# A three-layer transformer step: weight halves behind the norms, context keys and values beside a norm, q's second chunk rotated beside the first heads

## The chip, the cores and the metric

The kernel runs on one core of one Trainium2 chip. It is timed as a whole: device microseconds of one execution, median of several runs.

## The reference

An input of 256 tokens by 1024 goes through two layers and then through a third with a context of another 256 tokens:

```python
h = h + mix(rms_norm(h))         # layer a: dilated window attention; layer b: gated linear attention
h = h + swiglu(rms_norm(h))      # each with a gated FFN behind it
...
hx = modulate(rms_norm_2(x), sh1, sc1);  hc = modulate(rms_norm_2(ctx), csh1, csc1)
k_x = apply_axial_rope(rms_norm_2(ak_x), cos, sin);  k_c = rms_norm_2(ak_c)      # 2 key heads of 128
q_x = apply_axial_rope(rms_norm_2(aq_x), cos, sin)                               # 8 query heads of 128
attn_x = softmax(q_x @ [k_c, k_x].T / sqrt(128)) @ [v_c, v_x]
```

The third layer adds a gated delta rule (GDN) over context and input, merges the two, and ends in an FFN with a short convolution. Context and input use the same weight columns for keys and values. All matrices are fp32.

## The kernel before

Every product is made of three TensorE products in a rounded format (`mm3`, lines 324 to 326): operands are split in a high part (rounded on ScalarE) and a low part (the rest, on VectorE). Weights come in halves of 4 x 128 rows by 512 columns. `Weights` streams them in one fixed order: `load` on the SP queue into 4 raw buffers, `hi` (line 189) on ScalarE into 3 high buffers, `lo` (line 195) on VectorE in place of the raw half. `hi` of half h waits until half h - 3 is used up, `load` until half h - 4 is. A chunk is two halves (512 weight columns). `chunk_tok` multiplies a chunk for tiles of 128 tokens (tiles 0 and 1 the input's, 2 and 3 the context's), 12 products of 512 columns per half and tile.

No order is planned by a program: each engine works through its instructions as they are written, and semaphores join the engines. `Stage()` notes the newest signal of each engine when it is made, and `meet(engine)` makes an engine wait for all of them; every stage begins with it.

A *seam* is the piece between two layers. The last chunk of a stage is multiplied tile by tile (`last_tok`, or the end of `ffn`), so that the norm of tile 0 can start before tile 1 is done. `Norm.on_act` (line 525 squares, 527 root) and `Norm.on_dve` (532 reciprocal, 534 scale) stand behind the residual add of each tile (line 582 behind a mixer, 757 behind an FFN). Both halves of the next product (`nxt`) are rounded and split ahead of that, on ScalarE and on VectorE. Then `Norm.split` transposes the normed tiles on TensorE (line 405) into PSUM banks 4 to 7, after a wait for the last add, and splits them (ScalarE 423 or 414, VectorE 436, 443 or 452). Behind layer a, `GateWeights` is set up between the seam and the FFN: four DMA issues on ScalarE and a memset (line 1267) on VectorE; the stage of the FFN is noted behind it. Beside the FFN of layer b, `ContextNorm` norms and splits the context.

`attention_2` is the attention of the third layer. Chunk 0 gives keys and values for all four tiles (banks 0 to 3), chunks 1 and 2 give q (banks 4 to 7). Each is normed per head and rotated (`HeadNorm`): squares on ScalarE (856), sums (869), root (861), reciprocal (874), scale (878) and sine products (887) on VectorE, cosine products (900) and the add (905) on GpSimd. All three use the same buffers, so the squares of one wait for the add of the one before. Then comes a stage (`mid`), and behind it the heads: transposes of the keys (1688), a staging copy (1750), transposes of q (1725), and 16 units of scores (1697), maximum (1764, 1766), exponential (1744), transposes (1705), copy (1785, reciprocal 1786), values (1714) and result (1772). The units are in two groups of eight; the second group's q is copied, transposed and copied (1777) between them. The first two halves of the next stage, `gdn_inputs`, are rounded and split beside the q rotations.

## Time and profile before

| | |
|---|---|
| median of 3 runs | 1977.47 us (1976.63 to 1977.7) |
| the profiled execution | 1972.33 us |
| its span, first to last instruction | 1971.0 us |
| mean granted TensorE clock | 0.936 |
| TensorE products busy | 1701.1 us (86%), 10106 instructions |
| VectorE, ScalarE, GpSimd busy | 1143.7, 860.3, 238.5 us |
| DMA | 240.97 MB, mean 122 GB/s |

The profile is that of one execution. In a timeline row the first number is the start (us from the span's start), the second the time, and in brackets stand the engine's idle time ahead of it and what ended that. PE is the matrix engine TensorE, DVE VectorE, ACT ScalarE, POOL GpSimd. A window row gives the stretch, its length, the busy time of PE, PEld (weight loads), DVE, ACT and POOL with the number of instructions, then the granted TensorE clock, the share of DMA and GB/s.

### The profile page before, as it was taken

To read this page: it belongs to the slowest core of one execution; us is meant where nothing else is said; L and a number is where in the kernel's file an instruction comes from. 1 tells how busy PE (TensorE), PEld (TensorE's weight loads), DVE (VectorE), ACT (ScalarE), POOL (GpSimd) and SP (SyncE) were. 2 spreads that over 40 slices of the span, in tenths; PEclk is the share of its full clock that TensorE was granted. 3 is DMA by queue.
4 is the path that set the end of the run, shared out by engine and by line. 5 is a ranking of instruction groups with operands and counts; after the bars stand their busy time and mean duration, and the time that the engine had idled before them with its cause. 6 is when DMAs were issued, how large, how long until landed. Compare 5 with 4: busy or idle time off the path is not lost. (4 is left out here: it accounts for less than half of the span.)

```text
span 1971.0 us, 25094 instructions
## 1 busy us (share of the span) xinstructions
PE 1701.1 (86%) x10106; PEld 1479.6 (75%) x10106; DVE 1143.7 (58%) x1466; ACT 860.3 (44%) x1055; POOL 238.5 (12%) x200
## 2 busy tenths in 40 slices
PE   3998999879997986689997689967979979979988
PEld 2777888869986864579985568746979858769976
DVE  2887666745544456545544664427888555547754
ACT  4435556634434452344443234335544444335543
POOL 1553230000000000000001400002553200000000
PEclk9999999979998898789998889987989889989999
DMA  4553335536544352245543304100000055435533
GB/s 164 169 179 107 129 129 193 192 102 191 184 169 160 117 169 99 78 156 182 184 162 97 126 1 114 60 0 17 1 1 1 1 174 179 161 122 184 175 140 118
DMA packets 161906, 240.97 MB, mean 122 GB/s; under 512 B 12640, under 2 KB 80992, under 8 KB 161664
## 3 DMA queue, kind: packets, MB, share of 16 engines
q1 hardware_dynamic: 154400, 232.81, 36.2%
q10 hardware_dynamic: 7248, 5.77, 1.0%
q8 instruction: 81, 1.33, 0.3%
q0 software_dynamic: 144, 0.79, 0.1%
q14 instruction: 33, 0.27, 0.0%
HBM read 238.29 MB, written 1.05 MB: 121 GB/s over the span
## 5 line engine op out<-in xcount | busy, mean ns | idle before, releaser
L195 DVE TENSOR_TENSOR wlo<-raw,whi 128x2048 fp32r<-128x2048 f32 x224 | 523.9, 2351 | 361.7 <-ACT whi L189 348.5
L189 ACT ACTIVATE whi<-raw 128x2048 fp32r<-128x2048 f32 x224 | 420.1, 1886 | 352.3 <-PE ps L326 308.7
L324 PE MATMUL ps<-xs,whi 128*128 128x256 f32 (+1 forms) x1312 | 388.1, 296 | 17.7 <-DVE xs L443 5.1
L325 PE MATMUL ps<-xs,whi 128*128 128x256 f32 (+1 forms) x1312 | 386.5, 295 | 0.0
L326 PE MATMUL ps<-xs,wlo 128*128 128x256 f32 (+1 forms) x1312 | 386.2, 294 | 0.0
L324 PE MATMUL ps<-whi,xs 128*128 128x512 f32 x672 | 275.0, 409 | 35.3 <-DVE wlo L195 19.5
L324 PEld LDWEIGHTS ps<-xs,whi 128*128 128x128 f32 x1312 | 251.3, 192 | 27.3 <-issue 20.8
L325 PE MATMUL ps<-wlo,xs 128*128 128x512 f32 x672 | 269.6, 401 | 0.0
L326 PE MATMUL ps<-whi,xs 128*128 128x512 f32 x672 | 269.5, 401 | 0.0
L325 PEld LDWEIGHTS ps<-xs,whi 128*128 128x128 f32 x1312 | 251.3, 192 | 5.7
L326 PEld LDWEIGHTS ps<-xs,wlo 128*128 128x128 f32 x1312 | 251.0, 191 | 5.8
L324 PEld LDWEIGHTS ps<-whi,xs 128*128 128x128 f32 x672 | 129.3, 192 | 68.3 <-issue 36.7
L326 PEld LDWEIGHTS ps<-whi,xs 128*128 128x128 f32 x672 | 128.8, 192 | 32.0
L325 PEld LDWEIGHTS ps<-wlo,xs 128*128 128x128 f32 x672 | 129.3, 192 | 28.7
L324 PE MATMUL ps<-whi,hid 128*128 128x512 f32 x264 | 106.0, 402 | 8.7 <-DVE wide L728 8.7
L326 PE MATMUL ps<-whi,hid 128*128 128x512 f32 x264 | 105.5, 399 | 0.0
L325 PE MATMUL ps<-wlo,hid 128*128 128x512 f32 x264 | 105.4, 399 | 0.0
L1659 POOL TENSOR_TENSOR wide<-cst,wide 128x128 f32<-128x128 f32 x4 | 3.5, 863 | 789.5 <-DMA wide<-in_rows 789.5
L900 POOL TENSOR_TENSOR wide<-wide 128x512 f32<-128x512 f32 (+1 forms) x32 | 56.8, 1795 | 154.6 <-DVE wide L887 83.5
L905 POOL TENSOR_TENSOR wide<-wide 128x512 f32<-128x512 f32 (+1 forms) x32 | 72.1, 2275 | 3.4 <-DVE wide L887 2.4
L324 PEld LDWEIGHTS ps<-whi,hid 128*128 128x128 f32 x264 | 50.4, 191 | 21.0 <-DVE wide L728 9.1
L400 PE MATMUL ps<-cst,wide 128*128 128x128 f32 x112 | 20.0, 355 | 48.5 <-DVE wide L476 28.8
(360 smaller groups left out, 2423.9 us busy)
## 6 DMA issues: line engine op xcount, KB each, us to landing
raw<-in_ffn_w_gate_up SPq DMA_DIRECT2D x88, 512.0 KB, 4.7
raw<-in_a_w_in SPq DMA_DIRECT2D x72, 512.0 KB, 4.6
raw<-in_w_in SPq DMA_DIRECT2D x60, 512.0 KB, 4.6
raw<-in_w_mod SPq DMA_DIRECT2D x48, 512.0 KB, 4.6
raw<-in_w_up SPq DMA_DIRECT2D x44, 512.0 KB, 4.7
raw<-in_ffn_w_down SPq DMA_DIRECT2D x40, 512.0 KB, 4.5
raw<-in_b_w_in SPq DMA_DIRECT2D x24, 512.0 KB, 4.6
raw<-in_w_down SPq DMA_DIRECT2D x20, 512.0 KB, 3.9
```

Source lines behind the costliest of these rows:

```text
L189: self.hi_ok.inc(act.activation(self.whi[:, h % NHI, 0:nk, :], self.raw[:, h % NRAW, 0:nk, :], ACT.Copy))
L195: self.lo_ok.inc(dve.tensor_tensor(self.wlo[:, h % NRAW, 0:nk, :], self.raw[:, h % NRAW, 0:nk, :], self.whi[:, h % NHI, 0:nk, :].bitcast(F ...
L324: pe.matmul(o, ahi, bhi, start=start, stop=False)
L325: pe.matmul(o, ahi, blo, start=False, stop=False)
L326: return pe.matmul(o, alo, bhi, start=False, stop=stop)
L400: i_ = pe.transpose(ps[:, self.bank + g, (j * 2 + t) * P:(j * 2 + t + 1) * P], self.src(t, 2 * g + j), ident)
L900: i_ = pool.tensor_tensor(self.av[:, t], self.xv[:, t], bc(cos[:, t, :], 1, self.nh), ALU.mult)
L905: i_ = pool.tensor_tensor(dst(t), self.av[:, t], dst(t) if self.bv is None else self.bv[:, t], ALU.add)
L1659: pool.tensor_tensor(tab[:, 0, t, :], cosv[:, t, :], gain, ALU.mult)
```

## The change

At the seams, the second half of the next chunk is rounded behind the norm of both tiles and its low half is taken behind the split; `Norm` gets a bank of its own (4 for four of the norms, 0 for that between layer a's FFN and layer b), and the wait for the last add goes away, except in the seam ahead of the third layer. The FFN of layer a gets a stage that is noted ahead of `GateWeights`.

In the seam ahead of the third layer the products of the context's two tiles with the two halves of chunk 0 are made inside the seam (`context_first`): those with the first half ahead of the transposes, those with the second behind them. The low half of the second weight half is taken ahead of the split there. `attention_2` then makes only the input's two tiles of chunk 0.

In `attention_2` the three rotations get buffers of their own; the stage `mid` goes; the keys are transposed between the two halves of chunk 2; the first group of heads waits only for q's first chunk, and q's second chunk is rotated beside it: its cosine and sine products and the add on GpSimd. The 16 units run through, with the staging copy of the second group at unit 6 and its transposes and copy around units 6 and 7. The second half of the next stage is rounded behind the first staging copy and its low half taken in unit 2. What is computed stays the same. The core of the diff:

```diff
@@ -333,8 +333,10 @@
-    def chunk_tok(chunk, banks, tiles=(0, 1)):
-        for s, half in enumerate(chunk):
+    def chunk_tok(chunk, banks, tiles=(0, 1), parts=(0, 1), keep=False):
+        for s in parts:
+            half = chunk[s]
...
-            W.used.inc(i_)
+            if not keep:
+                W.used.inc(i_)
             self.root, self.ready = [0, 0], [0, 0]
-        def split(self):
-            parts = Split(lambda t, k: self.xn[:, t, k * P:(k + 1) * P], 0, self.stage, self.scale, self.shift, self.perm)
-            pe.wait_ge(added.sem, added.n)
+        def split(self, last, ahead=None):
+            parts = Split(lambda t, k: self.xn[:, t, k * P:(k + 1) * P], 0, self.stage, self.scale, self.shift, self.perm, self.bank)
+            if ahead is not None:
+                ahead(0)
+                pe.wait_ge(added.sem, added.n)
             for t in range(TT):
                 pe.wait_ge(st_ready.sem, self.ready[t])
                 parts.tile_on_pe(t)
+            W.hi(last)
             parts.on_act()
-            parts.on_dve()
+            if ahead is not None:
+                ahead(1)
+                W.lo(last)
+                parts.on_dve()
+            else:
+                parts.on_dve()
+                W.lo(last)
...
@@ -553,7 +568,7 @@
         def on_act():
-            for h in (*chunks[1], *nxt):
+            for h in (*chunks[1], nxt[0]):
-            for h in nxt:
-                W.lo(h)
+            W.lo(nxt[0])
...
         yb, zb = (c(2, 4, SEQ), c(2, 4, SEQ)) if conv is not None else (None, None)
-        at_, a0, v0, h0, l0, m0, y0 = Stage(), ff_act.n, ff_val.n, ff_hi.n, ff_lo.n, ff_y0.n, ff_y.n
-        order = [*up[1:], *down[0], *down[1], nxt]
+        at_ = at_ or Stage()
+        a0, v0, h0, l0, m0, y0 = ff_act.n, ff_val.n, ff_hi.n, ff_lo.n, ff_y0.n, ff_y.n
+        order = [*up[1:], *down[0], *down[1], nxt[:1]]
-        def squares(self, u, x):
-            if u:
+        def squares(self, u, x, own=False):
+            if u and not own:
                 act.wait_ge(hr_out.sem, u)
+            if sin is None:
+                return
...
+    def context_first(chunk, split, s):
+        pe.wait_ge(xs_hi.sem, split.hi0 + 4)
+        pe.wait_ge(xs_lo.sem, split.hi0 + 4)
+        want = list(xs_want)
+        xs_want[:] = [0, 0]
+        chunk_tok(chunk, (2, 3), (2, 3), (s,), keep=True)
+        xs_want[:] = want
...
+        def turned_on_pool():
+            r = rope_q[1]
+            pool.wait_ge(hr_xn.sem, x0 + 3)
+            for t in range(TT):
+                i_ = pool.tensor_tensor(r.av[:, t], r.xv[:, t], bc(tq[:, 0, t, :], 1, 4), ALU.mult)
+            hr_a.inc(i_)
+            for t in range(TT):
+                for c0 in (0, 64):
+                    halves = r.xv[:, t, :, c0:c0 + 64].rearrange("p h (s n) -> p h s n", s=2)[:, :, ::-1, :]
+                    i_ = pool.tensor_tensor(r.bv[:, t, :, c0:c0 + 64].rearrange("p h (s n) -> p h s n", s=2), halves,
+                                            bc(tq[:, 1, t, c0:c0 + 64], 1, 4).rearrange("p h (s n) -> p h s n", s=2), ALU.mult)
+            hr_a.inc(i_)
+            pool.wait_ge(hr_a.sem, a0 + 4)
+            for t in range(TT):
+                i_ = pool.tensor_tensor(q_to(1, t), r.av[:, t], r.bv[:, t], ALU.add)
+            hr_out.inc(i_)
+        def on_pe():
+            at_.meet(pe)
+            chunk_tok(chunks[0], (0, 1), (0, 1))
+            chunk_tok(chunks[1], (4, 5))
+            chunk_tok(chunks[2], (6, 7), parts=(0,))
+            pe.wait_ge(hr_out.sem, out0 + 1)
+            pe.wait_ge(c2_v.sem, 1)
             for g in range(KV2):
                 for t in range(NT2):
                     i_ = pe.transpose(ps[:, g, t * P:(t + 1) * P], k[:, t, g * HD2:(g + 1) * HD2], ident)
             c2_kt.inc(i_)
+            chunk_tok(chunks[2], (6, 7), parts=(1,))
+            q_transposes(0)
+            pe.wait_ge(c2_k.sem, 1)
+            scores(0)
+            for u in range(16):
+                if u < 15:
+                    scores(u + 1)
+                transposes(u)
+                if u:
+                    values(u - 1)
+                if u == 6:
+                    q_transposes(1)
+            values(15)
+        def q_transposes(g):
+            pe.wait_ge(c2_st.sem, g + 1)
+            pe.wait_ge(c2_k.sem, g)
+            for t in range(TT):
+                for h in range(GROUP2):
+                    i_ = pe.transpose(ps[:, 4 * (1 - g) + t, h * P:(h + 1) * P], stg[:, t, h * P:(h + 1) * P], ident)
+            c2_qt.inc(i_)
...
+        def values(u):
+            g, par = u // 8, u % 2
+            pe.wait_ge(c2_etv.sem, u + 1)
+            if u < 2:
+                pe.wait_ge(hr_xn.sem, x0 + 3)
+            else:
+                pe.wait_ge(c2_out.sem, u - 1)
+            for j in range(NT2):
+                i_ = pe.matmul(ps[:, 6 + par, 0:P], ET[:, par, j * P:(j + 1) * P], v[:, j, g * HD2:(g + 1) * HD2],
+                               start=(j == 0), stop=(j == NT2 - 1))
...
+        def on_act():
+            at_.meet(act)
+            load_row(gk, "k_norm")
+            load_row(gq, "q_norm")
+            for h in chunks[1]:
+                W.hi(h)
+            W.wait_used(act, chunks[0][1])
+            rope_k.on_act(u0, ps[:, 0:4, 0:256])
+            act.wait_ge(hr_xn.sem, x0 + 1)
+            c2_v.inc(act.activation(v, ps[:, 0:4, 256:512], ACT.Copy))
+            for h in chunks[2]:
+                W.hi(h)
+            W.wait_used(act, chunks[1][1])
+            rope_q[0].squares(u0 + 1, q_of(0), own=True)
+            rope_q[0].root(u0 + 1)
+            W.hi(nxt[0])
+            act.wait_ge(hr_out.sem, out0 + 2)
+            c2_st.inc(act.activation(stg, q[:, :, 0:CW], ACT.Copy))
+            W.hi(nxt[1])
+            W.wait_used(act, chunks[2][1])
+            rope_q[1].squares(u0 + 2, q_of(1), own=True)
+            rope_q[1].root(u0 + 2)
+            for u in range(16):
+                if u == 6:
+                    act.wait_ge(hr_out.sem, out0 + 3)
+                    act.wait_ge(c2_qt.sem, 1)
+                    c2_st.inc(act.activation(stg, q[:, :, CW:2 * CW], ACT.Copy))
+                exponentials(u)
+        def on_dve():
+            at_.meet(dve)
+            for h in chunks[1]:
+                W.lo(h)
+            dve.wait_ge(c2_tab.sem, 1)
+            rope_k.on_dve(u0, ps[:, 0:4, 0:256], tk[:, 1])
+            for h in chunks[2]:
+                W.lo(h)
+            rope_q[0].on_dve(u0 + 1, q_of(0), tq[:, 1])
             dve.wait_ge(c2_kt.sem, 1)
             c2_k.inc(dve.tensor_copy(kT, ps[:, 0:2, :]))
+            W.lo(nxt[0])
+            rope_q[1].sums(u0 + 2)
+            rope_q[1].scale_and_sin(u0 + 2, q_of(1), None)
+            dve.wait_ge(c2_qt.sem, 1)
+            c2_q.inc(dve.tensor_copy(qT[:, 0], ps[:, 4:6, :]))
+            maxima(0)
+            for u in range(16):
+                par, n = u % 2, u % 8
+                if u == 7:
+                    dve.wait_ge(c2_qt.sem, 2)
+                    c2_q.inc(dve.tensor_copy(qT[:, 1], ps[:, 0:2, :]))
+                if u < 15:
+                    maxima(u + 1)
+                dve.wait_ge(c2_et.sem, u + 1)
+                dve.wait_ge(c2_exp.sem, u + 1)
+                dve.tensor_copy(ET[:, par, :], ps[:, 4 + par, :])
+                c2_etv.inc(dve.reciprocal(rl[:, n:n + 1], l[:, n:n + 1]))
+                if u == 2:
+                    W.lo(nxt[1])
+                if u:
+                    result(u - 1)
+            result(15)
...
-    layer_a(N["a_in"], N["a_out"], N["ffn_a"][0][0], Norm(4096, f_norm[:, 0, :]))
+    layer_a(N["a_in"], N["a_out"], N["ffn_a"][0][0], Norm(4096, f_norm[:, 0, :], bank=4))
+    ffn_stage = Stage()
     gw = GateWeights()
-    ffn(*N["ffn_a"], N["b_in"][0], Norm(3072, a_norm[:, 1, :]), beside=gw)
-    layer_b(N["b_in"], N["b_out"], N["ffn_b"][0][0], Norm(0, f_norm[:, 1, :]), gw)
+    ffn(*N["ffn_a"], N["b_in"][0], Norm(3072, a_norm[:, 1, :]), beside=gw, at_=ffn_stage)
...
-    ffn(*N["ffn_b"], N["akv"][0], Norm(3072, modcol[:, 1, :, 0], modcol[:, 0, :, 0]), beside=ContextNorm(ctx))
+    cn = ContextNorm(ctx)
+    ffn(*N["ffn_b"], N["akv"][0], Norm(3072, modcol[:, 1, :, 0], modcol[:, 0, :, 0], bank=4), beside=cn,
+        ahead=lambda s: context_first(N["akv"][0], cn.split, s))
```

In the lines left out, `exponentials`, `maxima`, `result`, `scores` and `transposes` are the functions of before, moved; `q_transposes` writes banks 4 and 5 for the first group, 0 and 1 for the second; and the other calls of `Norm` get `bank=4`.

## Rows read from the trace of the kernel before

**Rows 1.** The page of the kernel before: granted TensorE clock in its 40 slices

```profile
PEclk9999999979998898789998889987989889989999
```

**Rows 2.** The list of waits, TensorE: who was waited for, us in total, times, longest

```profile
PE ps L405 <- DVE resid L582: 20.1, 3, 8.1
...
PE ps L1688 <- POOL wide L905: 18.0, 1, 18.0
```

**Rows 3.** The timeline (start, us) and a window row, the fifth seam

```profile
1051.29 1.92 ACT L189 ACTIVATE whi<-raw 128x2048 fp32r<-128x2048 f32 x1 [5.12 <-PE ps L326]
...
1053.30 2.29 DVE L195 TENSOR_TENSOR wlo<-raw,whi 128x2048 fp32r<-128x2048 f32 x1 [4.74 <-ACT whi L189]
...
1058.60 0.68 DVE L757 TENSOR_TENSOR resid<-resid,ps 128x512 f32<-128x512 f32 x1
...
1059.34 1.97 PE L405 MATMUL ps<-cst,wide 128*128 128x128 f32 x8 [6.75 <-DVE resid L757]
...
1066.19 2.48 DVE L443 TENSOR_TENSOR xs<-wide,xs 128x512 fp32r<-128x512 f32 x4
...
1068.88 0.76 PE L324 MATMUL ps<-whi,xs 128*128 128x512 f32 x1 [5.08 <-DVE xs L443]
...
1068.90:1073.00 4.10, 4.10 (x10) 3.23 (x11) 1.19 (x1) 1.91 (x1) 0.69 (x1) 0.51 0.13 32
```

**Rows 4.** The timeline, TensorE: transposes and restart at the other four seams

```profile
425.03 1.97 PE L405 MATMUL ps<-cst,wide 128*128 128x128 f32 x8 [6.63 <-DVE resid L582]
...
433.93 0.55 PE L324 MATMUL ps<-xs,whi 128*128 128x256 f32 x1 [4.44 <-DVE wide L1267]
...
632.86 1.97 PE L405 MATMUL ps<-cst,wide 128*128 128x128 f32 x8 [8.03 <-DVE resid L757]
...
640.38 0.39 PE L324 MATMUL ps<-xs,wzs 128*32 128x256 f32 x1 [3.06 <-DVE xs L452]
...
850.69 1.97 PE L405 MATMUL ps<-cst,wide 128*128 128x128 f32 x8 [5.35 <-DVE resid L582]
...
858.22 0.55 PE L324 MATMUL ps<-xs,whi 128*128 128x256 f32 x1 [3.32 <-DVE xs L452]
...
1748.96 1.97 PE L405 MATMUL ps<-cst,wide 128*128 128x128 f32 x8 [8.09 <-DVE resid L582]
...
1758.50 0.55 PE L324 MATMUL ps<-xs,whi 128*128 128x256 f32 x1 [5.08 <-DVE xs L443]
```

**Rows 5.** The timeline and a window row: projections and rotations of the attention

```profile
1093.39 1.03 ACT L856 ACTIVATE wide<-ps 128x1024 f32<-128x1024 f32 x1 [9.23 <-PE ps L326]
...
1101.61 5.03 DVE L195 TENSOR_TENSOR wlo<-raw,whi 128x2048 fp32r<-128x2048 f32 x2
...
1112.94 3.63 DVE L887 TENSOR_TENSOR wide<-wide 128x256 f32<-128x256 f32 x4
...
1116.71 6.45 POOL L905 TENSOR_TENSOR wide<-wide 128x512 f32<-128x512 f32 x2 [0.76 <-DVE wide L887]
...
1131.15 2.48 POOL L905 TENSOR_TENSOR wide<-wide 128x512 f32<-128x512 f32 x2 [0.76 <-DVE wide L887]
...
1093.40:1115.60 22.20, 22.20 (x96) 17.66 (x94) 17.05 (x23) 10.88 (x9) 12.45 (x10) 1.00 0.59 190
```

**Rows 6.** The timeline: the 16 units of the heads, and the stage behind them

```profile
1140.48 2.08 PE L1697 MATMUL ps<-wide 128*128 128x512 f32 x2 [1.31 <-DVE wide L1777]
...
1145.14 0.69 DVE L1785 COPY wide<-ps 128x512 f32<-128x512 f32 x1
...
1149.29 0.69 DVE L1785 COPY wide<-ps 128x512 f32<-128x512 f32 x1
...
1158.06 0.69 DVE L1785 COPY wide<-ps 128x512 f32<-128x512 f32 x1
...
1167.46 0.69 DVE L1785 COPY wide<-ps 128x512 f32<-128x512 f32 x1 [0.70 <-PE ps L1705]
...
1184.28 0.36 PE L324 MATMUL ps<-xs,whi 128*128 128x256 f32 x1 [0.60 <-PE ps L1714]
```

More of the change, by code:

```diff
@@ L624, in build, with ffn @@
     DOWN = ((0, (HK, HK)), (8, (HK, HK)), (16, (HK, 2)))
-    def ffn(up, down, nxt, norm, conv=None, gate=None, beside=None):
+    def ffn(up, down, nxt, norm, conv=None, gate=None, beside=None, at_=None, ahead=None):
         c = Carve(end=arena_n - 2 * FT * SEQ)
@@ L762, in ffn @@
         on_dve()
-        norm.split()
+        norm.split(*nxt[1:], **({} if ahead is None else {"ahead": ahead}))
     md_sil, md_hi, md_rows = (Signal(nc, "act", "mod_" + n) for n in ("silu", "hi", "rows"))
@@ L1241, in split_and_add @@
         prod_dve()
-        norm.split()
+        norm.split(nxt[1])
     lb_w = Signal(nc, "dma", "b_gate_weights")
@@ new lines, in scores, with transposes @@
+        def scores(u):
+            g, h, t, par = u // 8, u % 8 // 2, u % 2, u % 2
+            if u % 8 < 2:
+                pe.wait_ge(c2_q.sem, g + 1)
+            if u >= 2:
+                pe.wait_ge(c2_exp.sem, u - 1)
+            c2_sc.inc(pe.matmul(ps[:, 2 + par, :], qT[:, g, t, h * P:(h + 1) * P], kT[:, g, :], start=True, stop=True))
+        def transposes(u):
+            par = u % 2
+            pe.wait_ge(c2_exp.sem, u + 1)
+            if u >= 2:
+                pe.wait_ge(c2_etv.sem, u - 1)
+            for j in range(NT2):
+                i_ = pe.transpose(ps[:, 4 + par, j * P:(j + 1) * P], E[:, par, j * P:(j + 1) * P], ident)
+            c2_et.inc(i_)
```

188 lines of the change are left out of this document (46 added, 142 removed).

## The prediction

> **What bounds the kernel now.** I read the page first: the clock line of its slices [rows 1] shows TensorE at its upper level wherever it is kept busy, and below it only in some slices. So TensorE is the bound, except where it waits. The list of TensorE's waits [rows 2] shows on whom: 20.1 us in three waits of the norms' transposes (line 405) for the residual add of line 582 (two more, for the add of line 757, are like it), and 18.0 us in one wait of the attention's first transposes (line 1688) for GpSimd's last rope add. Then I read the timeline at these places. There are five seams, where a layer's last product is added, normed, transposed, split and only then multiplied: layer a to its FFN, that to layer b, b to its FFN, that to the keys and values of the context layer, and the mixer c to its FFN.
>
> **How a seam works** [rows 3, 4]. At 1051.29 ScalarE rounds the *second* weight half of the next product. It could not start earlier: its buffer is that of the last product's first half. The squares of token tile 0 are queued behind it, VectorE's low half (1053.30, 2.29 us) too, although the products of tile 0 were done 18 products before the end. The add of tile 1 follows at 1058.60, 6.0 us after the last product ended (1059.34 less 6.75 is 1052.6). TensorE starts again at 1068.88, at half clock: the granted clock is 0.51 for 4.1 us, that is 1.2 GHz. 96 products at the full pace (22.20 us for 96, 0.231 each, [rows 5]) would take 22.3 us; these end at 1093.3, after 24.4. So the restart costs 2 us more.
>
> **The change, part by part: four seams.** The second half moves behind the norm (rounding on ScalarE, low half behind the split on VectorE); the transposes go to banks that nobody reads, so tile 0's no longer wait for the add of tile 1. Tile 0's chain (add, squares, root, scale; 3.1 us, 4.4 with a table load, longer by two products with the gate in c) now runs beside tile 1's products, and the add of tile 1 starts about 0.2 us after the last product. In [rows 4] the transposes start 0.73 us behind that add, so it starts at 424.3, 632.1, 850.0, and with c's gate (one product more) 1747.5; the last products ended at 418.4, 624.8, 845.3 and 1740.9. In the seam to layer b tile 0's chain is late: add at 620.8, done at 625.4, so the second add starts there 0.5 us behind the products. It comes earlier by 5.7, 6.8, 4.4 and 6.4 us. Against this: every later stage waits for the *newest* signal of each engine. Behind the split that is now the low half of 2.29 us, so TensorE's restart pays it in full: the wait that takes the place of the one removed. ScalarE's rounding (1.9 us) holds the split up by 0.15, and nothing in c. In the first seam the stage of the FFN is noted ahead of the gate weights, so the memset (the wait of 4.44 us on line 1267) no longer stands before TensorE: 1.4 us. Net: 5.7 - 2.3 - 0.2 + 1.4 = 4.6; 6.8 - 2.3 - 0.2 = 4.3; 4.4 - 2.3 - 0.1 = 2.0; 6.4 - 2.3 = 4.1. Sum 15.0 us. The half clock after each restart I leave as it is: pauses of 5.3 us bring it already [rows 4], and about 6 us of waiting remain. If one such restart were spared it would give 2 us; so 0 to 8 more.
>
> **The fifth seam** also gets work. Of the 96 products of the first chunk 48 are for the context, whose split is long done. 24 (5.6 us) stand ahead of the transposes, 24 behind them. From 1052.6: products to 1058.2. The add of tile 1 is at 1052.8 and its chain done at 1056.0, rounding to 1057.0, low half to 1059.4 (ahead of the split here): all covered. The transposes (16, 2.0 us at full clock, 3.9 at half) 1058.2 to 1060.3; modulation and split on VectorE, 3.7 + 2.5 us as now, to 1065.8; beside them the other 24 products to 1065.9. TensorE thus never pauses long enough to lose its clock. The 48 latent products end at 66.0 + 11.2 = 1077.3 instead of 1093.4: 16.1 us earlier. Uncovered, the first 24 would cost up to the 2.2 us by which they outlast the norm; that is in the sum.
>
> **From there to the first score.** Now it takes 1140.5 - 1093.4 = 47.1 us. Keys and values keep their course [rows 5]: squares, root, scale, sine, and VectorE's two low halves end 13.2 us behind the chunk, so at 1090.5. TensorE meanwhile has chunk 1 (11.1 us, to 1088.5) and half of chunk 2 (to 1094.1); the low half of that is due at 1088.2, which is just in time (0 to 1 us). The first q squares have buffers of their own and no longer wait for GpSimd's add: sums start at 1090.6, where they started 3.2 us behind the low halves before. Sums to the end of the sine take 6.8 us: 1097.4. Then GpSimd's add. Alone the pair takes 2.48 us; beside two low halves it took 6.45; now a copy and one low half run beside it: I take 4.5, the middle, so 1102.1, with 2.5 and 6.5 as ends. Staging copy 1.06, transposes 1.0. ScalarE, behind the copy, rounds a half (1.9) and squares q's second chunk (1.03); VectorE sums, root, reciprocal, scale (3.1): 1109.3; its copy of the turned q 1.22; first score at 1110.7. From the chunk's end that is 33.4 us instead of 47.1: 13.7 us saved.
>
> **The heads.** 16 units; VectorE is the bound in each, the copies of line 1785 at 1149.29 and 1158.06 are four units apart, 2.19 us each [rows 6]. Between the groups the pipeline drains: 1145.14 to 1167.46 is 22.3 us for 8 units, 4.8 more than 17.5. In its place come a copy of 1.22 and one score that it holds up, about 2.1: a gain of 2.7; the low half moved into unit 2 costs 2.3. Net 0.4 us. GpSimd now turns q's second chunk itself: 3 us of cosines, 4 sine products that no row shows on it. Nearest: its cosine product of the same 128x256 shape, 0.78 us; at the worst 1.7, its add of that shape beside low halves. So 3 to 7 us, then the add, 2.5 to 6.5: done between 1118 and 1126. ScalarE asks for it at unit 6, at 1110.7 + 2.1 + 13.1 + 2.3 = 1128.2. Hidden, with 2 us to spare at the worst by these rows.
>
> At this add a rule of the Trainium skill bears (SBUF — State Buffer, section Who interferes with whom): a VectorE instruction with two SBUF inputs and a GpSimd one that reads SBUF exclude each other for a whole instruction. This trace agrees (6.45 against 2.48 us). By that rule the add waits out one low half, 2.48 + 2.3 = 4.8, and the sum is 0.3 us smaller.
>
> A rule that speaks against moving the sine: GPSIMD Engine Reference, section Performance versus the Vector engine, gives tensor_tensor on GpSimd as 1.96 times as long as on VectorE. VectorE's four sine products take 3.6 us here, so by that page 7.1 us, an estimate; the sum would stay, and the spare at unit 6 is what it eats.
>
> **Sum:** 15.0 + 16.1 + 13.7 + 0.4 = 45.2 us. The profiled execution took 1972.3 us (span 1971.0 and 1.3 around it), so 1927.1 for its like; the median of the runs is 5.1 us above it, so 1932.3 for the median. That is the forecast.
>
> **The rivals.** (1) *Unit 6 waits for GpSimd.* For it: no row shows the reversed product there, and the add beside VectorE takes up to 3.2 us an instruction. If all eight instructions took 3.3 us, it would end at 1109.3 + 26.4 = 1135.7, ScalarE's copy at 1136.8, and the heads would stand for 8.5 us: 1941. Against it: the cosines took 1.5 each. (2) *The context products are not hidden* (the low half late, or the norm behind them): half of them, 5.6, to all, 11.2 us, come back: 1938 to 1943.5. Against it: the working above, with 0.9 us between low half and the end of the transposes. (3) *The clock is spared* at the seams: two to four restarts without the half clock, 4 to 8 us more: 1924 to 1928. For it: transposes of tile 0 follow the products at once. Against it: 6 us of waiting remain. (4) *The seams give nothing*, as the low half and the rounding eat all: 1947. Against it: they cost 2.4 of 4.4 to 6.8. (5) *Slower:* the granted clock. TensorE's rests go away; if the chip answered more work with its lower level for longer, each 1% of mean clock would cost about 17 us (1701 us busy). From a mean of 0.91 instead of 0.936 on it would eat the gain, at 0.90 the kernel would be slower, near 1990. Against it [rows 1, 5]: the clock is 1.00 in all stretches where TensorE has been busy throughout. (6) *The change doesn't do what it says*: another stage still waits on a newer signal. Within 0.2%, 1977.
>
> **How the numbers follow.** Forecast 0.66, (1) 0.09, (2) 0.07, (3) 0.10, (4) 0.04, (5) 0.02, (6) 0.02. Bounds of the unknown costs around 1932.3: down 2.0 (the add alone), 8 (clock), 2 (noise); up 2.0 (the add), 1 (first half of chunk 2), 2 (four seams), 2 (noise), 5 (pipeline of the heads disturbed by copy, transposes and low half). They are not all due at once; together with rivals (1) to (3) the range 1921 to 1944 leaves about 2 in 10 out. A measurement here can tell about 0.2%, 4 us. Faster by more: all but (5) and (6), 0.96; within: 0.02; slower: 0.02.
>
> **What would show it.** In the new trace: at four seams the add of tile 1 within 1 us of the last product, and TensorE released not by the split but by the low half (line 195); if it is released by the split, the seam gains 2.3 more. In the fifth no pause above 1 us and clock 1.00 through it. The first score 33 us behind the chunk's end, released by VectorE's copy. Unit 6 and 7 without a wait on GpSimd. Units still at 2.19 us. The forecast is wrong if a unit lengthens, if GpSimd's second rotation takes over 19 us, or if the mean clock falls.

## The result, and the profile of the changed kernel

The changed kernel takes 1928.33 us (median of 4 executions, 1925.72 to 1930.22), the kernel before beside it 1977.05. The ratio is 0.9753, with an interval of 0.9736 to 0.977: between 45.5 and 52.2 us less, 48.7 by the medians. Forecast were 1932.3 in a range of 1921 to 1944. The profiled execution took 1925.72 us, its span 1924.4 (before 1971.0: 46.6 less); the sum of the prediction was 45.2.

Where the 46.6 us lie, place by place in the two traces (all in us):

| place | before | after | gain | predicted |
|---|---|---|---|---|
| seam a to FFN, last product's end to restart | 15.53 | 10.42 | 5.1 | 4.6 |
| seam to layer b | 15.55 | 10.64 | 4.9 | 4.3 |
| seam b to FFN | 12.87 | 10.42 | 2.45 | 2.0 |
| seam c to FFN | 17.62 | 13.00 | 4.6 | 4.1 |
| fifth seam, last product's end to the first chunk's end | 40.8 | 24.8 | 16.0 | 16.1 |
| chunk's end to first score | 47.1 | 33.1 | 14.0 | 13.7 |
| first score to the stage behind the heads | 43.8 | 43.4 | 0.4 | 0.4 |
| everything the change doesn't touch | | | -0.8 | 0 |

The page of the changed kernel, its busy times, then its granted clock in 40 slices, which answers to [rows 1]:

```profile
PE 1689.2 (88%) x10106; PEld 1470.5 (76%) x10106; DVE 1138.4 (59%) x1462; ACT 859.3 (45%) x1055; POOL 240.9 (13%) x204
...
PEclk9999999989999898789999899978989989989989
```

What went is mostly waiting: of the 46.6 us, 34.7 are idle time of TensorE and 11.9 busy time (1701.1 us before). The same 10106 products took less because more of them ran at the upper clock; between the last product of the FFN and the end of the first chunk of the fifth seam alone TensorE was busy for 28.5 us before and for 24.6 after. The list of TensorE's waits of the changed kernel (who was waited for, us in total, times, longest), which answers to [rows 2]:

```profile
PE ps L324 <- DVE wlo L195: 47.5, 18, 13.6
...
PE ps L408 <- DVE wide L538: 10.3, 5, 3.1
...
PE ps L1733 <- DVE wide L1808: 6.0, 1, 6.0
```

The waits of the transposes for the residual add and of the heads for GpSimd are gone. In their place stand the low half of line 195 (22.9 us in 14 waits before), the last scale of the norm (line 538) and VectorE's copy of the turned q (line 1808).

One of the four seams, layer a to its FFN, in the timeline of the changed kernel (start, duration, engine, line, operation; in brackets the idle time before and who ended it), which answers to [rows 4]:

```profile
421.98 1.04 PE L408 MATMUL ps<-cst,wide 128*128 128x128 f32 x8
...
422.18 0.69 DVE L596 TENSOR_TENSOR resid<-resid,ps 128x512 f32<-128x512 f32 x1 [1.07 <-PE ps L326]
...
424.28 1.90 ACT L189 ACTIVATE whi<-raw 128x2048 fp32r<-128x2048 f32 x1
...
425.41 1.22 PE L408 MATMUL ps<-cst,wide 128*128 128x128 f32 x8 [2.40 <-DVE wide L538]
...
426.93 3.22 DVE L455 SCALAR_TENSOR_TENSOR xs<-ps,vec,xs 128x256 fp32r<-128x256 f32 x8 [1.57 <-ACT xs L426]
...
430.07 2.28 DVE L195 TENSOR_TENSOR wlo<-raw,whi 128x2048 fp32r<-128x2048 f32 x1
...
432.56 0.55 PE L324 MATMUL ps<-xs,whi 128*128 128x256 f32 x1 [5.93 <-DVE wlo L195]
```

Tile 0's transposes run as the last products end (422.14), with the add of tile 1 beside them and not in front of them. The rounding fits between the norm's root and the transposed values. The split is done at 430.15, and TensorE could go; it goes 2.4 us later, released by the low half. The other three seams end in the same way. The transposes of tile 0 and the restart in the seam to layer b, and the restart in c's:

```profile
623.79 1.09 PE L408 MATMUL ps<-cst,wide 128*128 128x128 f32 x8 [0.41 <-DVE wide L538]
...
634.03 0.39 PE L324 MATMUL ps<-xs,wzs 128*32 128x256 f32 x1 [5.85 <-DVE wlo L195]
...
1710.80 0.55 PE L324 MATMUL ps<-xs,whi 128*128 128x256 f32 x1 [7.90 <-DVE wlo L195]
```

The fifth seam of the changed kernel, timeline and then a window row (stretch, its length, busy time and count of PE, PEld, DVE, ACT and POOL, granted clock, DMA share, GB/s), which answer to [rows 3]:

```profile
1042.83 0.69 DVE L773 TENSOR_TENSOR resid<-resid,ps 128x512 f32<-128x512 f32 x1 [0.96 <-PE ps L326]
...
1046.95 2.29 DVE L195 TENSOR_TENSOR wlo<-raw,whi 128x2048 fp32r<-128x2048 f32 x1 [0.92 <-ACT whi L189]
...
1048.25 1.91 PE L408 MATMUL ps<-cst,wide 128*128 128x128 f32 x16
...
1055.96 0.47 PE L324 MATMUL ps<-whi,xs 128*128 128x512 f32 x1 [0.18 <-issue]
...
1042.60:1056.00 13.40, 13.22 (x66) 10.61 (x64) 10.01 (x16) 5.79 (x8) 0.00 (x0) 1.00 0.46 156
```

TensorE is busy for 13.22 of 13.40 us between the last product of the FFN and the first of the latents, at a clock of 1.00, and the rest of the chunk, to 1067.4, has 1.00 too. Before, that stretch was a pause, and the restart ran at 0.51.

From the chunk's end to the first score, timeline of the changed kernel, which answers to [rows 5] and the first of [rows 6]:

```profile
1063.86 2.93 POOL L1666 TENSOR_TENSOR wide<-cst,wide 128x32 f32<-128x32 f32 x4
...
1067.43 1.03 ACT L872 ACTIVATE wide<-ps 128x1024 f32<-128x1024 f32 x1 [3.62 <-PE ps L326]
...
1068.79 1.22 DVE L885 TENSOR_REDUCE wide<-wide 128x8 f32<-128x1024 f32 x1 [2.52 <-POOL wide L1669]
...
1083.97 3.62 DVE L905 TENSOR_TENSOR wide<-wide 128x256 f32<-128x256 f32 x4
...
1087.73 4.57 POOL L923 TENSOR_TENSOR wide<-wide 128x512 f32<-128x512 f32 x2 [0.77 <-DVE wide L905]
...
1088.65 2.53 DVE L195 TENSOR_TENSOR wlo<-raw,whi 128x2048 fp32r<-128x2048 f32 x1
...
1099.16 1.21 DVE L1808 COPY wide<-ps 128x1024 f32<-128x1024 f32 x1
...
1100.52 3.75 PE L1733 MATMUL ps<-wide 128*128 128x512 f32 x4 [5.99 <-DVE wide L1808]
```

And the second rotation, which now runs on GpSimd beside the first heads, with ScalarE's copy of its result for unit 6:

```profile
1099.32 2.48 POOL L1680 TENSOR_TENSOR wide<-wide 128x512 f32<-128x512 f32 x2 [7.02 <-DVE wide L894]
...
1101.76 2.77 POOL L1685 TENSOR_TENSOR wide<-wide 128x256 f32<-128x256 f32 x4
...
1104.61 2.49 POOL L1690 TENSOR_TENSOR wide<-wide 128x512 f32<-128x512 f32 x2
...
1115.86 1.05 ACT L1782 ACTIVATE wide<-wide 128x1024 f32<-128x1024 f32 x1
```

It takes 7.8 us in all and is done at 1107.1, 8.8 us before it is asked for.

### The profile page after: what moved, and what is told of

It reads as the page before. It is cut to its first block and busy times, and to the rows that moved or that the text cites. A ratio compares the mean times of both kernels' runs of the same rounds, so it can differ in the third digit from the quotient of the medians.

```text
span 1924.4 us, 25090 instructions
## 1 busy us (share of the span) xinstructions
PE 1689.2 (88%) x10106; PEld 1470.5 (76%) x10106; DVE 1138.4 (59%) x1462; ACT 859.3 (45%) x1055; POOL 240.9 (13%) x204
## 5 line engine op out<-in xcount | busy, mean ns | idle before, releaser
L324 PE MATMUL ps<-whi,xs 128*128 128x512 f32 x672 | 275.9, 411 | 29.5 <-DVE wlo L195 18.7
L918 POOL TENSOR_TENSOR wide<-wide 128x512 f32<-128x512 f32 (+1 forms) x30 | 54.0, 1822 | 135.0 <-DVE wide L905 83.2
L923 POOL TENSOR_TENSOR wide<-wide 128x512 f32<-128x512 f32 (+1 forms) x30 | 67.7, 2280 | 2.6 <-DVE wide L905 1.7
```

What stands on the lines that cost most here:

```text
L324: pe.matmul(o, ahi, bhi, start=start, stop=False)
L918: i_ = pool.tensor_tensor(self.av[:, t], self.xv[:, t], bc(cos[:, t, :], 1, self.nh), ALU.mult)
L923: i_ = pool.tensor_tensor(dst(t), self.av[:, t], dst(t) if self.bv is None else self.bv[:, t], ALU.add)
```

## The experiments

Each edit is one to the changed kernel, unless it says otherwise. The ratio is the kernel's time over that of the kernel before, run on the same chip; the changed kernel itself has 0.9753, and 0.9752 with an interval of 0.9737 to 0.9766 when it was run again.

### Does each part give what the trace says?

**The four seams as before** (both halves ahead of the norm, the old wait, the stage noted behind the gate weights; the fifth seam and the attention stay changed):

```
-                pe.wait_ge(added.sem, added.n)
+            pe.wait_ge(added.sem, added.n)
...
-            W.hi(last)
+            if ahead is not None:
+                W.hi(last)
...
-                W.lo(last)
...
-            for h in (*chunks[1], nxt[0]):
+            for h in (*chunks[1], *nxt):
...
-            W.lo(nxt[0])
+            for h in nxt:
+                W.lo(h)
...
-        order = [*up[1:], *down[0], *down[1], nxt[:1]]
+        order = [*up[1:], *down[0], *down[1], nxt if ahead is None else nxt[:1]]
...
-    ffn(*N["ffn_a"], N["b_in"][0], Norm(3072, a_norm[:, 1, :]), beside=gw, at_=ffn_stage)
+    ffn(*N["ffn_a"], N["b_in"][0], Norm(3072, a_norm[:, 1, :], bank=4), beside=gw)
```

> The changed kernel with four seams as before (both halves of the next chunk ahead of the norm, a wait for the last add, layer a's FFN noted behind its gate weights); the fifth seam and the attention stay changed. Theory: the seams gave 16.6 us in the trace (last product to restart: 15.5, 15.6, 12.9, 17.6 us before, 10.6, 10.7, 10.6, 13.2 after), so 1928.3 + 16.6 = 1945. Rival (seam times are luck of the clock, the rest of the stages gives it back): under 1938.

Measured: 1946.26 us, ratio 0.9852 (0.9839 to 0.9866). The four pauses are 15.49, 15.54, 12.90 and 17.64 us, as before; all 17.1 us are back. By the ratios it is 0.0099, 19.5 us; their intervals leave about 15 to 24. So the seams give what the traces show, some 17 us, and nothing else in the kernel gives it.

**The context products back behind the norm.** No products run ahead in the fifth seam, and the attention's first chunk has all 96 again:

```
             if ahead is not None:
-                ahead(0)
                 pe.wait_ge(added.sem, added.n)
...
-                ahead(1)
                 W.lo(last)
...
-            chunk_tok(chunks[0], (0, 1), (0, 1))
+            chunk_tok(chunks[0], (0, 1, 2, 3), (0, 1, 2, 3))
```

> The changed kernel with the context's 48 products back in the attention's first chunk. Theory: they cost their 11.2 us, and TensorE's pause of some 10 us in the seam brings the half clock back for 2 us: 1928.3 + 13.2 = 1941.5; the restart stays 13.2 to 13.4 us behind the last product, as the low half and VectorE's split set it. Rival (the products delayed the norm, so taking them out lets TensorE restart 2.2 us earlier): 1939. Rival (they were not hidden): within 5 us of 1928.

Measured: 1937.85 us, ratio 0.9812 (0.9797 to 0.9828), 0.0059 above the changed kernel: 11.7 us. Its timeline, restart and chunk's end:

```profile
1053.64 0.76 PE L324 MATMUL ps<-whi,xs 128*128 128x512 f32 x1 [7.42 <-DVE xs L446]
...
1078.25 1.03 ACT L870 ACTIVATE wide<-ps 128x1024 f32<-128x1024 f32 x1 [9.22 <-PE ps L326]
```

The last product of the FFN ends at 1040.97 here; the restart comes 12.67 us behind it, 0.7 earlier than with the context products between, and then at half clock: 24.6 us for 96 products where the full pace is 22.3. The chunk ends 37.3 us behind the last product instead of 24.8. So 12.5 of the 16 us are the filled pause with its spared restart. The other 3.5 are what the rest of the change gives in this seam, the second half rounded behind the norm; this part is the difference, and no run takes it back alone. The expectation of 13.2 left out the 0.7 us that the restart comes earlier when no context products stand in front of the transposes; its rival had 2.2 us for that.

**The heads wait for q's second chunk again.** How much of the attention's gain is that they no longer do? The first transposes of q wait again until the rotation of the *second* chunk is done too:

```
             pe.wait_ge(c2_st.sem, g + 1)
+            if g == 0:
+                pe.wait_ge(hr_out.sem, out0 + 3)
```

> The changed kernel, but TensorE turns the first q chunk only when GpSimd has rotated the second one too (one wait more). Theory: GpSimd's last add ends 7.8 us behind VectorE's scaling of the second chunk, at 1107.1 in the trace; transposes (1 to 2 us), copy 1.2: first score at 1109.4 to 1110.5 instead of 1100.5, so 9 to 10 us more: 1938. Rival (the first score waits mainly for something else, the copy or ScalarE): under 4 us more.

Measured: 1936.7 us, ratio 0.9803 (0.9783 to 0.9823). In its timeline:

```profile
1102.39 1.94 PE L1726 MATMUL ps<-cst,wide 128*128 128x128 f32 x8 [16.53 <-issue]
...
1105.74 3.75 PE L1735 MATMUL ps<-wide 128*128 128x512 f32 x4 [1.41 <-DVE wide L1810]
```

From the chunk's end, at 1062.55 here, to the first score it takes 43.2 us instead of 33.1. So 10.1 us of the 14.0 come from the heads not waiting for the second chunk. (After 16.5 us of waiting the transposes run at half clock, 1.94 us instead of 1.09.)

**The second chunk's sine on VectorE again**, in front of the copy that releases the first score:

```
-            turned_on_pool()
+            rope_q[1].on_pool(u0 + 2, tq[:, 0], lambda t: q_to(1, t))
...
-            rope_q[1].scale_and_sin(u0 + 2, q_of(1), None)
+            rope_q[1].scale_and_sin(u0 + 2, q_of(1), tq[:, 1])
```

> The changed kernel with the sine products of q's second chunk on VectorE again. Theory: they stand between VectorE's scaling and its copy of the first turned q chunk, 3.6 us as in the other rotations, and the first score waits for that copy: 3.6 us more from the chunk's end to the first score (36.7 instead of 33.1), and GpSimd's last add ends about 1 us sooner, of no use. In all 1928 + 3.6 = 1932. Rival (GpSimd's turn is what unit 6 waits for, and VectorE does it faster): no change or a gain.

Measured: 1931.6 us, ratio 0.9765 (0.9746 to 0.9784). Chunk's end (1067.58) to first score:

```profile
1104.35 3.75 PE L1733 MATMUL ps<-wide 128*128 128x512 f32 x4 [9.59 <-DVE wide L1808]
```

36.8 us, so 3.7 more than 33.1: the four sine products stand before VectorE's copy. They take VectorE 3.56 us here because GpSimd's cosine products run beside them: two of the four take 1.48 us, the other two 0.42. So the move spares VectorE not only the work but also a collision of about 2.1 us. The time of the whole kernel cannot tell 3.7 us: its interval overlaps that of the changed kernel.

**The first q squares wait for the rotation of the keys, as before:**

```
-            rope_q[0].squares(u0 + 1, q_of(0), own=True)
+            rope_q[0].squares(out0 + 1, q_of(0))
```

> The changed kernel, but the squares of q's first chunk wait for GpSimd's add of the keys, as they had to with shared buffers. Theory: the add ended at 1082.9 in the trace, VectorE's sums began at 1080.8; squares take 1.03, so the sums begin 3.2 us later and all behind them too: 33.1 + 3.2 = 36.3 us from the chunk's end to the first score, 1931.5 in all. Rival (VectorE's low halves or the tables set the course): no change.

Measured: 1931.19 us, ratio 0.9775 (0.9757 to 0.9793). The squares now stand for GpSimd's add, and the score comes 36.4 us behind the chunk's end (1068.62), 3.3 more:

```profile
1084.28 1.03 ACT L872 ACTIVATE wide<-ps 128x1024 f32<-128x1024 f32 x1 [6.31 <-POOL wide L923]
...
1105.01 3.75 PE L1733 MATMUL ps<-wide 128*128 128x512 f32 x4 [5.11 <-DVE wide L1808]
```

So buffers of its own give the q chunk 3.3 us. If the two add up, which no run shows, 3.3 and 10.1 are 13.4 of the 14.0.

### Which part of the seam change does the work?

**The wait for the last add put back** at all four seams, everything else changed. This tells whether the free banks are part of the gain:

```
             if ahead is not None:
                 ahead(0)
-                pe.wait_ge(added.sem, added.n)
+            pe.wait_ge(added.sem, added.n)
```

> The changed kernel with the wait for the last add back ahead of the transposes of tile 0, at the four seams; the second weight half stays behind the norm. Theory: of the two edits at a seam this one is worth next to nothing: the add of tile 1 ends 0.9 us behind the last product, tile 0's transposes (1 us) are then done long before tile 1 is ready, 3.4 us behind the last product. 0 to 0.3 us a seam: within 1.5 us of the changed kernel. Rival (the banks are what freed the seam): 5 to 15 us more.

Measured: 1927.35 us, ratio 0.9757 (0.9741 to 0.9773). In the first seam:

```profile
420.55 1.09 PE L408 MATMUL ps<-cst,wide 128*128 128x128 f32 x8 [0.78 <-DVE resid L596]
...
423.05 1.09 PE L408 MATMUL ps<-cst,wide 128*128 128x128 f32 x8 [1.40 <-DVE wide L538]
...
430.19 0.55 PE L324 MATMUL ps<-xs,whi 128*128 128x256 f32 x1 [6.06 <-DVE wlo L195]
```

Tile 0's transposes do come 0.8 us behind the last product, after the add. But tile 1's have to wait for their own scale anyway (1.40 us), and the pauses are 10.42, 10.64, 10.42 and 13.01, the same as without the wait. The missing wait gains nothing, and with it the free banks. Only the seam to layer b writes other banks than before in any case (0 to 3 instead of 4 to 7); at the other three the transposes went to banks 4 to 7 already, which the mixer's last products (0 to 3) do not use, and only the wait kept them back.

**Both halves ahead of the norm again**, with banks, absent wait and early stage kept:

```
-            W.hi(last)
+            if ahead is not None:
+                W.hi(last)
...
-                W.lo(last)
...
-            for h in (*chunks[1], nxt[0]):
+            for h in (*chunks[1], *nxt):
...
-            W.lo(nxt[0])
+            for h in nxt:
+                W.lo(h)
...
-        order = [*up[1:], *down[0], *down[1], nxt[:1]]
+        order = [*up[1:], *down[0], *down[1], nxt if ahead is None else nxt[:1]]
```

> The changed kernel with both weight halves ahead of the norm again at the four seams; banks, the missing wait for the add and the early stage of layer a's FFN stay. Theory: the place of the second half is what gave the seams their 17.1 us, but for the memset of the gate weights (1.4): 14.5 to 15.7 us more than the changed kernel. Rival (the banks did it): under 5 us more.

Measured: 1941.29 us, ratio 0.9818 (0.9804 to 0.9833); pauses 14.16, 15.55, 12.88, 17.63, in sum 60.2, 15.7 more. The first seam in its timeline:

```profile
418.98 2.29 DVE L195 TENSOR_TENSOR wlo<-raw,whi 128x2048 fp32r<-128x2048 f32 x1 [6.11 <-ACT whi L189]
...
425.56 0.68 DVE L597 TENSOR_TENSOR resid<-resid,ps 128x512 f32<-128x512 f32 x1
...
428.79 1.97 PE L408 MATMUL ps<-cst,wide 128*128 128x128 f32 x8 [1.12 <-DVE wide L538]
...
430.38 3.23 DVE L455 SCALAR_TENSOR_TENSOR xs<-ps,vec,xs 128x256 fp32r<-128x256 f32 x8 [1.65 <-ACT xs L426]
...
433.82 0.55 PE L324 MATMUL ps<-xs,whi 128*128 128x256 f32 x1 [3.06 <-DVE xs L455]
```

So the order of the halves is the whole gain, except 1.4 us in the first seam (15.53 against 14.16) for the stage that no longer stands behind the gate weights. With the low half in front, even tile 0's add waits for it (421.19), so there is nothing to transpose into the free banks.

### What the new wait costs

**The low half is not counted as VectorE's newest signal**, so the next stage waits for the split alone:

```
+                kept = Signal.newest["dve"]
                 W.lo(last)
+                Signal.newest["dve"] = kept
```

> The changed kernel, but the stage behind a seam does not see the signal of the last low half (TensorE still waits for it at the products that read it). Theory: the low half of 2.29 us stands in full between split and restart at four seams, so TensorE restarts 2.2 us earlier at each, released by the split: 1928.3 - 9 = 1919. Rival: the wait moves on, to the second weight half or to the other engines' next stage, and less than 4 us are seen: 1925 to 1928.

Measured: 1915.26 us, ratio 0.9699 (0.9686 to 0.9713), 0.0054 below the changed kernel: 10.7 us. Pauses 8.23, 8.45, 8.22, 10.80: 2.2 less in each, 8.8 in sum. The first seam:

```profile
429.05 0.55 PE L324 MATMUL ps<-xs,whi 128*128 128x256 f32 x1 [3.85 <-DVE xs L455]
```

TensorE is released by the split. So the low half, which the prediction charged with 2.3 us in every seam, is a real cost of the changed kernel (2.2 us), and an avoidable one: TensorE needs that half only some products later, and has its own wait for it.

**In addition, the stage is noted ahead of the split**, so the first products start when half of the split is done, by their own waits:

```
+            self.ahead_of_split = Stage()
             parts = Split(lambda t, k: self.xn[:, t, k * P:(k + 1) * P], 0, self.stage, self.scale, self.shift, self.perm, self.bank)
...
-    ffn(*N["ffn_a"], N["b_in"][0], Norm(3072, a_norm[:, 1, :]), beside=gw, at_=ffn_stage)
+    ffn(*N["ffn_a"], N["b_in"][0], Norm(3072, a_norm[:, 1, :]), beside=gw, at_=norm_a.ahead_of_split)
```

The FFNs of layers b and c are given the stages of their own norms in the same way.

> The kernel whose stages do not see the last low half (measured at 1915.3), and at the three seams into an FFN the stage is noted ahead of the split: TensorE starts the first half as soon as two of the four groups are split. Theory: two groups of VectorE's last part are 1.6 us where it scales and subtracts and 1.2 us where it only subtracts, so 1.6 + 1.6 + 1.2 = 4.4 us less: 1911. Rival (the second half, with its low half behind the split, is then late): 1915.

Measured: 1912.76 us, ratio 0.9681 (0.9666 to 0.9696). Pauses 6.60, 8.52, 6.60 and 9.53, 4.5 us less than with the last edit alone; the seam to layer b keeps its stage.

```profile
429.74 0.55 PE L324 MATMUL ps<-xs,whi 128*128 128x256 f32 x1 [2.23 <-DVE xs L455]
```

The trace shows the 4.5 us; by the ratios it is 0.0018, 3.6 us, and the intervals overlap. Against the changed kernel the two edits together are beyond doubt: 0.9681 to 0.9753.

**On top of both, GpSimd's add is kept clear of VectorE's low half**: VectorE rounds it only when the add is done, and ScalarE's rounding moves behind the second q root.

```
             c2_k.inc(dve.tensor_copy(kT, ps[:, 0:2, :]))
+            dve.wait_ge(hr_out.sem, out0 + 2)
             W.lo(nxt[0])
...
-            W.hi(nxt[1])
...
             rope_q[1].root(u0 + 2)
+            W.hi(nxt[1])
```

> The same kernel as the one before it, with two moves in the attention: VectorE's low half that ran beside GpSimd's add of q's first chunk waits until that is done, and ScalarE squares the second chunk ahead of rounding the next weight half. Theory: the add then takes 2.5 us instead of 4.57 (what the rotation of the kernel before shows with VectorE idle), 2.1 less, and the squares start 1.9 us sooner: 33.1 - 4.0 = 29.1 us to the first score, 1907 in all. Rival (the add is as long as before, since it is not the low half that slows it): 31.2.

> The kernel with all four moves once more, as its place against its forerunner was within the spread: by the theory 29.5 us from the chunk's end to the first score and 3.6 us under the kernel without the two moves of the attention, 1909; by the rival (what the chain gives comes back in the heads) 1913.

Measured: 1911.92 us (ratio 0.9673, 0.9655 to 0.9691) and, run again, 1912.61 (0.9677, 0.966 to 0.9693). The add and its surroundings in the first of the two:

```profile
1075.99 2.54 POOL L926 TENSOR_TENSOR wide<-wide 128x512 f32<-128x512 f32 x2 [0.76 <-DVE wide L908]
...
1085.16 3.75 PE L1736 MATMUL ps<-wide 128*128 128x512 f32 x4 [4.39 <-DVE wide L1812]
```

The add takes 2.54 us with nothing beside it, 4.57 with one low half. The low half follows it at 1078.57. The first score comes 29.5 us behind the chunk's end (1055.63), and 29.6 in the second trace, against 33.1. So the chain is 3.5 us shorter, twice, where 4.0 were expected; 2.0 of it are the add, and that the rest is ScalarE's earlier squares is not shown by itself. The time of the whole kernel does not show it: 0.9673 and 0.9677 beside 0.9681, where 1907 and 1909 us had been expected. The heads have their 43.6 and 43.3 us in the two traces, so it isn't given back there. The stage behind them, whose own instructions neither move changes, took 554.7 us in the kernel before the two moves and 554.2 and 560.5 in these two traces of one kernel, so it differs by more than the gain. Whether the gain is lost in this spread stays open.

**The changed kernel itself, once more:**

> The changed kernel itself once more, beside the others on one chip: 1928, the four seams at 10.4, 10.6, 10.4 and 13.0 us by either theory; what its spans differ by from run to run lies in stages that no kernel here touches (the granted clock of the GDN stage).

Measured: 1927.81 us, ratio 0.9752 (0.9737 to 0.9766), pauses 10.42, 10.65, 10.45 and 13.00. The pauses of a seam repeat to within 0.03 us from trace to trace, so they tell edits apart that the whole time, with its 0.15%, cannot.

## Why the prediction was right, point by point

**What bounds the kernel.** TensorE, except where it waits: of the 46.6 us that the span lost, 34.7 were waits, and its busy time fell by 11.9, since fewer of the same products ran at the lower clock. That the waits come from the parts of the change is shown by undoing single parts, each of which brings its own waits back.

**Four seams: right mechanism, terms too small by 2.1 us** (15.0 predicted, 17.1 measured, 0.5 in each). The add of tile 1 does come at once, TensorE is released by the low half, and the seam to layer b has tile 0's chain a little late (0.41 us). Three small terms were mis-sized: the place of the add ("about 0.2 us after the last product"), the rounding (0.15, in the sums 0.2) and the low half (2.3). Put beside the trace with both halves in front, the first seam splits up so:

- The add starts 5.9 us behind the last product with the halves in front, and 0.04 changed: 5.86 us, where I had 5.7.
- From the add to VectorE's part of the split it is 4.82 us in front and 4.75 changed. I had charged 0.15 for the rounding. It costs nothing: ScalarE does it at 424.28, while the scale and the transposes of tile 1 run, and its own first transposed value comes 0.67 us behind the start of the transposes instead of 0.72. That is 0.2 us.
- From the split's start to the restart it is 3.44 and 5.63: the low half costs 2.2, not 2.3.

Together 0.5 us. The other three seams divide up in the same way. Against the kernel before, the add comes 7.03, 4.57 and 6.58 us earlier (6.8, 4.4 and 6.4 charged), the way from the add to the split is 0.08, 0.07 and 0.25 us shorter (0.2, 0.1 and 0 had been charged against it), and the low half costs 2.2 us in each.

The prediction also names the transposes on banks that nobody reads, "so tile 0's no longer wait for the add". That they no longer wait is true and worth nothing (pauses equal with the wait put back), since tile 1's transposes wait for tile 1's scale in any case; and in three of the four seams the banks did not change.

**Fifth seam: right** (16.1 and 16.0; restart 13.4 behind the last product in both). The clock was 1.00 throughout. The first 24 products do outlast the norm. The part of the context products alone is 12.5 us, by the experiment that put them back.

**Chunk's end to first score: right** (13.7 and 14.0). GpSimd's add took 4.57 us, for which I had taken 4.5 between ends of 2.5 and 6.5. The estimate by the rule of the Trainium skill (SBUF — State Buffer, section Who interferes with whom) was 4.8. The add takes 2.54 us clear of a low half and 4.57 with one beside it, a difference of 2.0 where a low half lasts 2.3, so the trace agrees. Two collisions of the same kind I had not seen: GpSimd's first table product (128x128, at 1059.29) met a low half and took 2.13 us instead of 0.46, and four small ones (128x32) met the next and took 2.93 instead of 0.87, so VectorE began the sums of the keys 0.3 us late.

**Heads: the net is right** (0.4 and 0.4), **its terms are not, and that they cancel is luck.** The copy between the groups is there (1121.14, 1.23 us) and so is the low half in unit 2 (1110.11, 2.27 us). Read from VectorE's copies (lines 1785 and 1819), the three intervals around the change of groups went from 11.06 to 9.03 us, a gain of 2.0 where 2.7 was predicted. The first five intervals, with the low half in them, went from 10.73 to 12.05, a cost of 1.3 where 2.3 was charged. And from the first score to the first of these copies it is 5.0 us instead of 4.7.

**The rivals.** (1) *Unit 6 waits for GpSimd*: no, it has 8.8 us to spare. The sine products that no row had shown took 2.77 us for the four, just under my bounds of 3 to 7, and nothing slowed the add (2.49). The 3.6 us that I took as VectorE's price of the four was not the price of the products alone: two of them ran beside GpSimd's cosines and took 1.50 us each, the other two 0.42 (rows in the last section). Product by product and clear of each other it is 0.72 us on GpSimd against 0.42 on VectorE, 1.7 times. The Trainium skill (GPSIMD Engine Reference, section Performance versus the Vector engine) has 1.96 times; the trace points the same way with a smaller ratio for this small shape. My estimate of 7.1 us by that page came out too long because it started from the 3.6. (2) *The context products are not hidden*: no. The low half ended at 1049.24, 0.9 us before the end of the transposes, as worked out. (3) *The clock is spared at the four seams*: no. Behind the restart of the first seam the granted clock is 0.50 in the changed kernel, and even in the version whose last wait is only 2.23 us; this is 1.2 GHz. (4) *The seams give nothing*: no, 17.1. (5) *Slower by the clock*: the mean rose from 0.936 to 0.947. (6) *It doesn't do what it says*: it does.

The window rows for (3) (columns as above), first of the changed kernel, then of the version with the stage ahead of the split:

```profile
432.60:436.00 3.40, 3.40 (x16) 3.40 (x17) 0.91 (x1) 1.21 (x1) 0.00 (x0) 0.50 0.66 193
```

```profile
429.80:433.00 3.20, 3.20 (x15) 3.20 (x16) 3.20 (x5) 0.29 (x1) 0.00 (x0) 0.50 0.17 28
```


**What the median adds.** The sum was 45.2; the places give 47.4, and the stretches between them take 0.8 back: up to the first seam 3.7 us longer, layer b 2.1 shorter, its FFN 0.9 longer, layer c behind the heads 2.7 shorter, the tail 1.1 longer. No edit is in them, and their clock differs (last section); that this is all of it was not tested. The median of the changed kernel lies 2.6 us above its profiled execution, for which I had added 5.1. So the 4.0 us between forecast and result are 1.4 of the sum (2.1 of the seams, less what the other stretches took) and 2.5 of that distance.

## What to carry to other kernels

Where a stage waits for the newest signal of an engine, any work queued behind what the stage needs becomes a part of its wait: here 2.2 us in each of four seams, which went when the weight half's signal was left out (8.8 us in the trace, 10.7 by the ratios of the whole). Order work at a seam by what the next engine waits for (residual add and norm first, the weights' second half behind them), and fill the pause that remains with products whose operands have long been there; that gave 12.5 us in one seam, 2.3 of it by sparing the restart at half clock. And take the price of an instruction from a row in which the other engine is quiet: a group of four that takes 3.62 us here holds two that were held up for 1.1 us each.

## What the runs showed of the hardware that was not expected

**The granted clock swings in stretches that no edit touches.** In the stage of layer c that follows the heads, two stretches of 50 us, each at the same distance from the stage's start. The last version (the two edits at the seams and the two moves in the attention), in its first run:

```profile
1278.80:1328.80 50.00, 39.00 (x257) 34.73 (x257) 36.05 (x62) 26.54 (x61) 18.47 (x15) 0.83 0.05 17
...
1478.80:1528.80 50.00, 38.27 (x324) 36.85 (x323) 26.90 (x74) 22.71 (x71) 5.56 (x5) 0.99 0.06 14
```

The very same kernel, run again:

```profile
1282.00:1332.00 50.00, 39.69 (x216) 34.30 (x216) 32.66 (x57) 24.89 (x59) 15.06 (x13) 0.71 0.05 17
...
1482.00:1532.00 50.00, 45.40 (x346) 43.72 (x344) 25.68 (x71) 21.34 (x71) 8.14 (x7) 0.90 0.00 1
```

0.83 and 0.99 against 0.71 and 0.90, with the same code; as the second execution gets on at another pace, a stretch at the same distance holds other products (216 instead of 257 in the first). The whole stage lasted 554.2 us in the first run and 560.5 in the second. It was 553.9 and 556.2 in the two traces of the changed kernel, 556.6 before, and between 553.9 and 560.5 in all fourteen traces. Layer a has such a place too, in the changed kernel at 76 to 96 us, with 0.91, where the kernel before had 1.00.

So two executions of one kernel differ by 6.3 us in one stage, more than the 3.5 us that the last two edits gave in the chain to the first score. What decides between the levels in these sparse stretches was not found.

**VectorE and GpSimd hold each other up, product by product.** VectorE's four sine products (128x256, reversed halves) of q's first chunk take 3.62 us as a group. One by one they take 0.43, 1.50, 1.51 and 0.41 us; beside the middle two run GpSimd's cosine products. The first two in the changed kernel:

```profile
1083.97 0.43 DVE L905 TENSOR_TENSOR wide<-wide 128x256 f32<-128x256 f32 x1
1084.31 1.50 DVE L905 TENSOR_TENSOR wide<-wide 128x256 f32<-128x256 f32 x1
```

GpSimd's two cosine products (128x512) take 2.96 us there, and 2.48 in the second chunk, where VectorE does no such products beside them; its four sine products then take 0.72 us each, 2.77 together. So 2.77 against 3.62 does not make GpSimd the faster engine for them: clear of each other VectorE needs 0.42 us for one. It also means that about 2.2 us of collision are left in q's first chunk, which is in the chain to the first score. How much of that another order could get back was not tested.

**A collision with a low half stretches even small GpSimd work**: four products of 128x32 took 2.93 instead of 0.87 us, nearly all of the difference in one of them (2.31 instead of 0.25), and two additions of 128x512 took 4.57 instead of 2.54. VectorE's low half itself grew from 2.29 to 2.53 beside that add, and to 2.83 beside the add of the keys.
